# Weight rows laid out in neighbouring pairs, 8 KB per descriptor, in a two-layer mLSTM / attention / mixture-of-experts kernel

## The chip, the cores and the metric

The kernel runs on one core of one Trainium2 chip. The metric is the device time of one execution in microseconds (us), median of 3 runs before the change.

## The reference, cut to what matters

There are 256 tokens of width 1024, all in float32, and two layers. Layer 0 is an mLSTM mixer (a projection to q, k, v, o and gates, then an output projection) and a mixture of experts. Layer 1 projects one shared K/V, then does windowed attention (query and output projections) and a second mixture of experts. After each half there is a LayerNorm of alpha * h + f(h). Of this computation, what the change touches is how the sums over the 1024 (or 512) input features are cut up:

```
proj = x @ w_in                                   # 1024 x 3080, mLSTM
mix  = h @ w_out                                  # 1024 x 1024
k, v = split(x @ w_kv)                            # 1024 x 512
q    = x @ w_q                                    # 1024 x 1024
probs = softmax(t @ w_router)                     # 1024 x 16
for e in range(16):                               # 16 experts, in each of 2 layers
    g, u = split(t @ w_gu[e])                     # 1024 x 1024
    y = (silu(g) * u) @ w_down[e]                 # 512 x 1024
    out += gate[:, e] * y
```

A sum over features may be taken in any order, as long as row r of the weight meets feature r of the other operand.

## The kernel before

**Layout.** A matmul sums over the 128 partitions of both its operands. The 1024 rows of a weight are therefore cut into 8 chunks of 128 (512 rows into 4): row k * 128 + p stands on partition p as chunk k. `big[0..3]` hold four 1024 x 1024 weights (4 MB each), `small[0..1]` two 512 x 1024 weights (2 MB each). The other operand of each product must have feature k * 128 + p on partition p too. It is made by TensorE: `turn` (L379) transposes 128 x 128 blocks of `h` into PSUM, from where ScalarE and VectorE copy them to `hT` (`take_hT`, L868 and L1071); and in the mixture of experts `gather` (L556) multiplies blocks of `h` by a 0/1 matrix `pick` that selects the tokens of two experts, giving `xe`. In both, a block of `h` of 128 neighbouring columns is the stationary operand, the one that a weight load brings into the array. The inner activations `act_g` (64 slots of tokens by 512, kept as 128 x 256) are transposed in the same way in `inner_T` (L590).

**Matmul instructions.** Each float32 matmul of the code shows in the trace as two MATMUL and two LDWEIGHTS instructions; a transpose shows as one of each.

**Weight traffic.** All weight loads are issued by SyncE in program order, in pieces of 1 MB, each with its own semaphore: `load_big` (L198) has four pieces of two chunks, `load_small` (L205) two. In such a piece each partition receives two rows of 4 KB that lie 128 rows apart in memory, as two descriptors of 4 KB. The first 1024 columns of `w_in` (q and k) come in four pieces of 256 columns (L215 to L218), with rows of 1 KB. A piece is issued as soon as the consumer of the buffer's former content is done (`wait_ge` on `gu_done`, `y_done` and the like), so the loads of the experts run about three experts ahead of their use in `big` and one in `small`. TensorE waits for a piece with `wait_big` (L374) or on the semaphores of `small` (L617).

**Order of the experts.** In both layers a turn of four experts is written out (`one_turn`, L637) and runs over four turns. Per expert TensorE does a gate/up product (L582), a transpose (L600), a down product (L619), and per pair of experts a `gather` (L564) and a `scatter` (L631).

**The start.** SyncE issues the two halves of `x`, then `w_in`. ScalarE's sequencer first issues four small DMAs (L865, L866: gate weights and gate biases), and only then reaches the first copies of `take_hT`, for which it loads an activation table. TensorE transposes `x` (L383) and then waits for `hT` and the first piece of `w_in` before the q/k product (L445).

Of the kernel before, what the change touches and what calls it, by code (L numbers as in the profile page):

```python
# [12 lines left out]
P = 128  # L13
NT = SEQ // P
KC = D // P
# [27 lines left out]
def build(nc, x, w_in_a, b_gates_a, mh_norm_a, w_out_a, w_kv_shared, w_q_b, sinks_b, w_out_b,  # L43
          w_router, b_router, w_gu, w_down, ln_g, ln_b, rope, out):
    ctx = ExitStack()
    with ctx:
# [150 lines left out]
        def _(sp):  # L197
            def load_big(n, src):  # L198

                buf, sems, _ = big_at(n)  # L200
                v = src.rearrange("(k p) n -> p k n", p=P)
                for q in range(4):
                    sp.dma_start(buf[:, 2 * q:2 * q + 2, :], v[:, 2 * q:2 * q + 2, :]).then_inc(sems[q], 16)

            def load_small(n, src):  # L205
                buf, sems, _ = small_at(n)
                v = src.rearrange("(k p) n -> p k n", p=P)
                for q in range(2):
                    sp.dma_start(buf[:, 2 * q:2 * q + 2, :], v[:, 2 * q:2 * q + 2, :]).then_inc(sems[q], 16)

# [4 lines left out]
            for q in range(4):  # L215
                sp.dma_start(big[0][:, :, q * 256:(q + 1) * 256],
                             w_in[:, q * 256:(q + 1) * 256].rearrange("(k p) n -> p k n", p=P)
                             ).then_inc(big_in[0][q], 16)  # L218
            load_big(1, w_in[:, 1024:2048])
            load_big(2, w_in[:, 2048:3072])  # L220
            load_big(3, w_out_a[0])
            for l in range(2):
# [10 lines left out]
                if l == 0:  # L233
                    load_dn(0)
                    load_dn(1)
                    sp.wait_ge(qk_done, 8)
                    load_gu(0)
                    sp.wait_ge(v_done, 4)
                    load_gu(1)
                    sp.wait_ge(o_done, 4)  # L240
                    load_gu(2)
                    sp.wait_ge(mix_done, 4)
                    load_gu(3)
                else:


                    sp.wait_ge(y_done, DONE - 1)
                    v = w_kv_shared.rearrange("(k p) n -> p k n", p=P)
                    buf, sems, _ = small_at(D_KV)
                    bv = buf[:, :, :].rearrange("p a (b n) -> p (a b) n", b=2)  # L250
                    for q in range(2):
                        sp.dma_start(bv[:, 4 * q:4 * q + 4, :], v[:, 4 * q:4 * q + 4, :]).then_inc(sems[q], 16)
                    sp.wait_ge(gu_done, DONE)
                    load_big(G_MIX[1], w_q_b[0])
                    load_big(G_MIX[1] + 1, w_out_b[0])
                    load_gu(0)
                    load_gu(1)
                    sp.wait_ge(y_done, DONE)
                    load_dn(0)
                    sp.wait_ge(q_done, 4)  # L260
                    load_gu(2)
                    sp.wait_ge(qT_done, 4)
                    load_dn(1)
                    sp.wait_ge(mix_done, 12)
                    load_gu(3)
# [10 lines left out]
                for e in (4, 5):  # L276
                    buf, sems, _ = big_at(G0 + e)
                    for q in range(4):
                        if q < 3:
                            sp.wait_ge(first_gu, 3 * (2 * l + e - 4) + q + 1)  # L280
                        else:
                            sp.wait_ge(gu_done, DONE + e - 3)
                        sp.dma_start(buf[:, 2 * q:2 * q + 2, :],
                                     w_gu[l, e].rearrange("(k p) n -> p k n", p=P)[:, 2 * q:2 * q + 2, :]
                                     ).then_inc(sems[q], 16)
# [14 lines left out]
                with sp.If(rounds > 0):  # L300
                    sp.wait_ge(s["dve"], 1)
                    with sp.Fori(0, rounds) as j:
                        with sp.Fori(0, EXPERTS) as e:
                            n0 = (j * EXPERTS + e) * (KC + FC)
                            for k in range(KC + FC):

                                sp.wait_ge(s["w_used"], n0 + (k + START))
                                src = (w_gu[l, bass.ds(e, 1), k * P:(k + 1) * P, :] if k < KC else
                                       w_down[l, bass.ds(e, 1), (k - KC) * P:(k - KC + 1) * P, :])
                                sp.dma_start(spill_w, src.rearrange("a p n -> (a p) n")).then_inc(s["w_in"], 16)  # L310

# [59 lines left out]
        def _(pe):  # L371
            mm = nc.tensor.matmul

            def wait_big(n, q, i=0):  # L374

                _, sems, fill = big_at(n)
                pe.wait_ge(sems[q], i * 16 + 16 * fill)

            def turn(src, n, t, j, bank0):  # L379

                for kk in range(4):
                    k = 4 * j + kk
                    last = nc.tensor.transpose(pb[bank0 + 2 * t + j][:, kk * P:(kk + 1) * P],  # L383
                                               src[:, t, k * P:(k + 1) * P], ident[:, :])
                last.then_inc(turned, 1)
# [54 lines left out]
            for g in range(8):  # L440
# [6 lines left out]
                last.then_inc(qk_done, 1)  # L447
            pe.wait_ge(gates_w_in, 64)
            for k in range(KC):
# [39 lines left out]
            for hd in range(M_HEADS):  # L489
# [5 lines left out]
                last.then_inc(num_done, 1)  # L495
            pe.wait_ge(params_in, 16 * 6)
            pe.wait_ge(rows_ready, 1)
# [23 lines left out]

            PAIRS_E = EXPERTS // 2

            def moe(l):
# [31 lines left out]
                def gather(m, P0, ks, bank=1):  # L556

                    for k in ks:
                        if k == 0:
                            pe.wait_ge(pick_ready, P0 + (m + 1))  # L560
                        if k % 4 == 0 and bank == 1:
                            pe.wait_ge(x_sb, (P0 + m) * 2 + (k // 4 - START))
                        for t in range(NT):
                            last = mm(pb[bank][:, (k % 4) * P:(k % 4 + 1) * P], h[:, t, k * P:(k + 1) * P],  # L564
                                      pick[m % 2][:, t, :, :].rearrange("p e s -> p (e s)"),
                                      start=t == 0, stop=t == NT - 1)
                        if k % 4 == 3:
                            last.then_inc(x_got, 1)
# [21 lines left out]
                def inner_T(u, E0, P0):  # L590
# [8 lines left out]
                    for j in range(2):  # L599
                        last = nc.tensor.transpose(pb[3][:, j * P:(j + 1) * P], act_g[u % 2][:, j * P:(j + 1) * P],  # L600
                                                   ident[:, :])
# [77 lines left out]
            def overflow(l):  # L679
# [3 lines left out]
                with pe.If(rounds > 0):  # L683
                    pe.wait_ge(s["dve"], 1)
                    with pe.Fori(0, rounds) as j:
                        with pe.Fori(0, EXPERTS) as e:
                            n = j * EXPERTS + e
                            pe.wait_ge(s["pick"], n + 1)
                            for half in range(2):
                                if half:  # L690
                                    pe.wait_ge(s["xs"], n * 2 + 1)
                                for k in range(4 * half, 4 * half + 4):
                                    for t in range(NT):
                                        last = mm(pb[1][:, (k % 4) * P:(k % 4 + 1) * P], h[:, t, k * P:(k + 1) * P],
                                                  pick[0][:, t, :, :].rearrange("p e s -> p (e s)"),
                                                  start=t == 0, stop=t == NT - 1)
                                last.then_inc(s["x"], 1)
# [10 lines left out]
                            for jj in range(2):  # L708
                                nc.tensor.transpose(pb[3][:, jj * P:(jj + 1) * P], act_g[0][:, jj * P:(jj + 1) * P],
                                                    ident[:, :])  # L710
# [137 lines left out]
        def _(act):  # L848
# [14 lines left out]
            for g in range(2):  # L863
                w4 = w_in_a[0, :, 3072 + g * M_HEADS:3072 + (g + 1) * M_HEADS]
                act.dma_start(w_gate[:, :, 32 * g:32 * g + M_HEADS], w4.rearrange("(k p) n -> p k n", p=P)).then_inc(gates_w_in, 16)  # L865
                act.dma_start(b_gate[32 * g:32 * g + M_HEADS, :],  # L866
# [17 lines left out]
            act.dma_start(rows[0][8:9], mh_norm_a).then_inc(rows_in, 16)  # L884
            act.dma_start(w_rt[:, :, :], w_router.rearrange("(k p) n -> p k n", p=P)).then_inc(params_in, 16)
            act.dma_start(b_rt[:, :], b_router.rearrange("(a n) -> a n", a=1).to_broadcast([P, EXPERTS])).then_inc(params_in, 16)
# [174 lines left out]
        def _(dve):  # L1061
# [46 lines left out]
            for t in range(NT):  # L1108
                take_hT(0, t, 4)
            dve.wait_ge(gates_w_in, 64)  # L1110
            V.tensor_scalar(b_gate[:, :], b_gate[:, :], 1.0 / CAP, None, ALU.mult).then_inc(d2a, 1)
# [53 lines left out]
            def route(l):  # L1165
# [4 lines left out]
                dve.wait_ge(logits, l + 1)  # L1170
                dve.wait_ge(params_in, 16 * 6)
                link(V.reduce_max(r_s[:, 0:2], pb[1][:, 0:32].rearrange("p (t e) -> p t e", t=NT), AX_X))
# [293 lines left out]
```

## Time and profile before

| | |
|---|---|
| median of 3 runs | 772.51 us (772.5 to 772.75) |
| span of the profiled execution (first to last instruction; its own time) | 773.3 us |
| TensorE (PE) busy | 741.0 us, 96% |
| weight loads (PEld) busy, beside PE | 350.1 us, 45% |
| VectorE, ScalarE, GpSimd busy | 171.5, 122.5, 22.3 us |
| DMA | 231.37 MB in 68163 packets, 299 GB/s over the span |

The first row is measured without the profiler, the others come from one profiled execution, whose span is 0.8 us above the median. PE is the matmul side of TensorE, PEld its weight loads, which overlap with matmuls; a busy PE says that it always had a matmul in flight, not that it ran at its peak.

### The profile page before, as it was taken

The page shows a single profiled execution, that of the slowest core. Times are in us where ns is not written, and L with a number is a line of the kernel's source. Part 1 is how long each engine was busy: PE and PEld are TensorE (multiplying, and loading weights), DVE is VectorE, ACT ScalarE, POOL GpSimd, SP SyncE. Part 2 cuts the span into 40 slices and gives each one's busy share as a digit, 9 for nine tenths or more (in the row PEclk, how much of TensorE's full clock was granted, in tenths as well). Part 3 has the DMA queues.
Part 4 walks back from the last instruction along what each step waited for, and adds up shares of the span by engine and source line. Part 5 has one row for each costly group of instructions (what it writes and reads, how often), then busy time and mean ns, then how long its engine had stood idle before and what let it go on. Part 6 is the DMA issues. An engine that isn't in the chain of part 4 may idle for free.

```text
span 773.3 us, 8287 instructions
## 1 busy us (share of the span) xinstructions
PE 741.0 (96%) x3270; PEld 350.1 (45%) x3270; DVE 171.5 (22%) x459; ACT 122.5 (16%) x286; POOL 22.3 (3%) x39
## 2 busy tenths in 40 slices
PE   5999999999999999999999999999999999999994
PEld 5845554554443443443334455455434434434331
DVE  0011121541111111101125354552111111011015
ACT  1122161111111110110122043211111101101002
POOL 3200100000000000000000021100000000000000
PEclk9999989999999999999999999999999999999998
DMA  9999305239699999989659928054979999999931
GB/s 280 390 410 360 146 1 217 81 137 389 237 411 410 409 409 410 409 349 409 256 198 409 409 102 326 1 217 178 366 284 408 410 409 410 410 384 371 389 109 56
DMA packets 68163, 231.37 MB, mean 299 GB/s; under 512 B 7961, under 2 KB 12057, under 8 KB 68130
## 3 DMA queue, kind: packets, MB, share of 16 engines
q1 hardware_dynamic: 63744, 230.70, 76.1%
q10 hardware_dynamic: 4386, 0.21, 0.5%
q8 instruction: 23, 0.38, 0.2%
q14 instruction: 10, 0.08, 0.0%
HBM read 229.85 MB, written 1.05 MB: 299 GB/s over the span
## 4 chain that ended last, share of the span: by engine, by line
PE 92%; DVE 3%; ACT 2%; ACTq 1%; issue 1%; POOL 1%; POOLq 0%; DVEq 0%
PE pb L582 29%; PE pb L413 17%; PE pb L619 15%; PE pb L564 8%; PE pb L631 7%; PE pb L445 4%; PE pb L546 2%; PE pb L751 2%; PE pb L600 1%; PE pb L493 1%; PE pb L532 1%; PE pb L383 1%; PE pb L789 1%; PE pb L390 1%; ACTq L866 1%
## 5 line engine op out<-in xcount | busy, mean ns | idle before, releaser
L413 PE MATMUL pb<-big,hT 128*128 128x512 f32 x320 | 142.5, 599 | 0.8 <-DVE hT L1415 0.8
L619 PE MATMUL pb<-small,bufC 128*64 128x512 f32 x512 | 116.9, 598 | 3.8 <-DVE bufC L1271 3.8
L582 PE MATMUL pb<-big,bufB 128*64 128x512 f32 x512 | 113.1, 594 | 0.0
L582 PE MATMUL pb<-big,hT 128*64 128x512 f32 x512 | 113.0, 594 | 0.0
L413 PEld LDWEIGHTS pb<-big,hT 128*128 128x128 f32 x320 | 59.9, 192 | 71.6 <-issue 69.7
L582 PEld LDWEIGHTS pb<-big,hT 128*64 128x64 f32 x512 | 36.1, 137 | 69.5 <-issue 68.5
L582 PEld LDWEIGHTS pb<-big,bufB 128*64 128x64 f32 x512 | 35.9, 137 | 68.6 <-issue 67.4
L619 PEld LDWEIGHTS pb<-small,bufC 128*64 128x64 f32 x512 | 33.9, 136 | 72.4 <-issue 65.4
L564 PEld LDWEIGHTS pb<-bufC,h 128*128 128x128 f32 x512 | 59.5, 192 | 15.0 <-issue 13.0
L1267 DVE TENSOR_TENSOR bufC<-bufC,pb 128x256 f32<-128x256 f32 x32 | 13.5, 421 | 236.4 <-ACT bufC L968 236.4
L564 PE MATMUL pb<-bufC,h 128*128 128x128 f32 x512 | 63.9, 279 | 0.3 <-DVE bufC L1235 0.3
L631 PE MATMUL pb<-bufB,v_shift 128*128 128x512 f32 x128 | 57.8, 594 | 0.9 <-DVE bufB L1279 0.9
L1279 DVE COPY bufB<-pb 64x512 f32<-64x512 f32 x32 | 21.9, 683 | 161.7 <-PE pb L619 161.7
L964 ACT ACTIVATE bufB<-pb 64x512 f32<-64x512 f32 x32 | 19.0, 593 | 160.9 <-PE pb L619 160.9
L968 ACT ACTIVATE bufC<-pb 128x256 f32<-128x256 f32 x32 | 12.3, 383 | 201.0 <-PE pb L582 201.0
L631 PEld LDWEIGHTS pb<-bufB,v_shift 128*128 128x128 f32 x128 | 23.1, 190 | 24.5 <-issue 23.0
L445 PE MATMUL pb<-hT,big 128*128 128x256 f32 x128 | 29.6, 396 | 3.4 <-ACT hT L872 3.4
L445 PEld LDWEIGHTS pb<-hT,big 128*128 128x128 f32 x128 | 25.4, 199 | 7.5 <-ACT hT L872 3.8
L367 POOL TENSOR_TENSOR bufA<-bufA,st 128x512 f32<-128x512 f32 x8 | 8.1, 1038 | 399.8 <-DVE st L1404 399.8
L600 PEld LDWEIGHTS pb<-ident,bufC 128*128 128x128 f32 x64 | 6.6, 140 | 24.5 <-issue 24.3
L957 ACT ACTIVATE bufB<-pb 128x512 f32<-128x512 f32 x16 | 9.6, 597 | 44.1 <-PE pb L564 44.1
L383 PE MATMUL pb<-ident,h 128*128 128x128 f32 x64 | 10.1, 312 | 5.4 <-DMA h<-in_x 4.4
(206 smaller groups left out, 447.6 us busy)
## 6 DMA issues: line engine op xcount, KB each, us to landing
big<-in_w_gu SPq DMA_DIRECT2D x128, 1024.0 KB, 13.9
small<-in_w_down SPq DMA_DIRECT2D x64, 1024.0 KB, 9.6
big<-in_w_in_a SPq DMA_DIRECT2D x12, 1024.0 KB, 15.5
big<-in_w_out_a SPq DMA_DIRECT2D x4, 1024.0 KB, 18.9
big<-in_w_q_b SPq DMA_DIRECT2D x4, 1024.0 KB, 14.5
big<-in_w_out_b SPq DMA_DIRECT2D x4, 1024.0 KB, 19.2
small<-in_w_kv_shared SPq DMA_DIRECT2D x2, 1024.0 KB, 6.9
h<-in_x SPq DMA_DIRECT2D x2, 512.0 KB, 3.9
```

The source lines that it names most:

```text
L383: last = nc.tensor.transpose(pb[bank0 + 2 * t + j][:, kk * P:(kk + 1) * P], src[:, t, k * P:(k + 1) * P], ident[:, :])
L413: last = mm(pb[bank][:, :], hT[:, k, t * P:(t + 1) * P], w[:, k, c * HALF:(c + 1) * HALF], start=k == 0, stop=k == KC - 1)
L445: last = mm(pb[g // 2][:, (g % 2) * SEQ:(g % 2 + 1) * SEQ], big[0][:, k, g * P:(g + 1) * P], hT[:, k, :], start=k == 0, stop=k == KC - 1)
L546: mm(pb[4 + 2 * t + c][:, :], alpha_i[:, :], h[:, t, c * HALF:(c + 1) * HALF], start=True, stop=False, skip_group_check=True)
L564: last = mm(pb[bank][:, (k % 4) * P:(k % 4 + 1) * P], h[:, t, k * P:(k + 1) * P], pick[m % 2][:, t, :, :].rearrange("p e s -> p (e s)"), s ...
L582: last = mm(pb[0][c * 64:(c + 1) * 64, :].rearrange("p (a n) -> p a n", a=2), xe[u // 2 % 2][:, k, (u % 2) * SLOTS:(u % 2 + 1) * SLOTS], w ...
L600: last = nc.tensor.transpose(pb[3][:, j * P:(j + 1) * P], act_g[u % 2][:, j * P:(j + 1) * P], ident[:, :])
L619: last = mm(pb[2][c * 64:(c + 1) * 64, :], heT[:, j * P + hf * 64:j * P + (hf + 1) * 64], w[:, kk, c * HALF:(c + 1) * HALF], start=(j, hf) ...
L631: ins = mm(pb[4 + 2 * t + c][:, :], back[:, t * P:(t + 1) * P], ye[:, c * HALF:(c + 1) * HALF], start=False, stop=last_one, skip_group_che ...
L751: last = mm(pb[4 + t][:, :], hT[:, k, t * P:(t + 1) * P], kvw[:, k, :], start=k == 0, stop=k == KC - 1)
L964: A(ye[p:p + 64, HALF:2 * HALF], pb[2][64:128, :], ACT.Copy).then_inc(y_sb, 1)
L1279: V.tensor_copy(ye[p:p + 64, 0:HALF], pb[2][0:64, :]).then_inc(y_sb, 1)
```

## The change

A 256-row group of a weight (what was two chunks) is laid out so that partition p holds rows 2p and 2p + 1 of the group. These lie next to each other in memory, so where whole rows are loaded a partition's part of a piece is one run of 8 KB. Chunk 2a + j then has feature 256a + 2p + j on partition p. The other operand follows: the blocks of `h`, of `val` and of `act_g` that are transposed or gathered are taken with every second column (`rows_of`, `half_of`), 128 columns with a step of 8 bytes where they were next to each other. `w_out_b`, whose other operand is the attention's output laid out by head, keeps the old layout (`load_big_by_head`). Pieces that are not whole rows (q/k columns of `w_in`, gate weights, router weights) are now issued as two DMAs of half the size, one for each j, with the counts of the waits adjusted. The K/V weight's rows are 2 KB, so its runs become 4 KB.

```
@@ load_big
-                v = src.rearrange("(k p) n -> p k n", p=P)
+                v = src.rearrange("(q p j) n -> p q j n", p=P, j=2)
                 for q in range(4):
-                    sp.dma_start(buf[:, 2 * q:2 * q + 2, :], v[:, 2 * q:2 * q + 2, :]).then_inc(sems[q], 16)
+                    sp.dma_start(buf[:, 2 * q:2 * q + 2, :], v[:, q]).then_inc(sems[q], 16)
@@ load_small: likewise, for q in range(2); w_gu of experts 4 and 5, w_kv_shared and the overflow path: likewise
@@ first piece of w_in
             for q in range(4):
-                sp.dma_start(big[0][:, :, q * 256:(q + 1) * 256],
-                             w_in[:, q * 256:(q + 1) * 256].rearrange("(k p) n -> p k n", p=P)
-                             ).then_inc(big_in[0][q], 16)
+                for j in range(2):
+                    sp.dma_start(big[0][:, :, q * 256:(q + 1) * 256].rearrange("p (a j) n -> p a j n", j=2)[:, :, j],
+                                 w_in[:, q * 256:(q + 1) * 256].rearrange("(a p j) n -> p a j n", p=P, j=2)[:, :, j]
+                                 ).then_inc(big_in[0][q], 16)
@@ TensorE
+            def rows_of(src, t, k):
+
+                return src[:, t, k // 2 * 256:(k // 2 + 1) * 256].rearrange("p (n j) -> p j n", j=2)[:, k % 2]
@@ turn
-                                               src[:, t, k * P:(k + 1) * P], ident[:, :])
+                                               rows_of(src, t, k), ident[:, :])
@@ gather
-                            last = mm(pb[bank][:, (k % 4) * P:(k % 4 + 1) * P], h[:, t, k * P:(k + 1) * P],
+                            last = mm(pb[bank][:, (k % 4) * P:(k % 4 + 1) * P], rows_of(h, t, k),
                                       pick[m % 2][:, t, :, :].rearrange("p e s -> p (e s)"),
@@ inner_T
+            def half_of(n, j):
+
+                return act_g[n].rearrange("p (n j) -> p j n", j=2)[:, j]
-                        last = nc.tensor.transpose(pb[3][:, j * P:(j + 1) * P], act_g[u % 2][:, j * P:(j + 1) * P],
+                        last = nc.tensor.transpose(pb[3][:, j * P:(j + 1) * P], half_of(u % 2, j),
                                                    ident[:, :])
@@ ScalarE, gate weights (the router's weights w_rt: likewise)
-                act.dma_start(w_gate[:, :, 32 * g:32 * g + M_HEADS], w4.rearrange("(k p) n -> p k n", p=P)).then_inc(gates_w_in, 16)
+                for j in range(2):
+                    act.dma_start(w_gate[:, :, 32 * g:32 * g + M_HEADS].rearrange("p (a j) n -> p a j n", j=2)[:, :, j],
+                                  w4.rearrange("(a p j) n -> p a j n", p=P, j=2)[:, :, j]).then_inc(gates_w_in, 16)
```

On TensorE the instructions stay the same in number and order, except for one register operation per pass through the loop of turns; what changes is the access pattern of the stationary operand. On two queues the instructions change. ScalarE's queue at the start of the program, before the change (`v_shift` is the memory in which the gate weights lie):

```order
L865 DMA v_shift<-in_w_in_a 128x8x4
L866 DMA b_gate<-in_b_gates_a 4x1
L865 DMA v_shift<-in_w_in_a 128x8x4
L866 DMA b_gate<-in_b_gates_a 4x1
L872 ACT_TABLE_LOAD
L872 ACTIVATE hT<-pb 128x4x128 x3
```

and with the change:

```order
L885 DMA v_shift<-in_w_in_a 128x4x4 x2
L887 DMA b_gate<-in_b_gates_a 4x1
L885 DMA v_shift<-in_w_in_a 128x4x4 x2
L887 DMA b_gate<-in_b_gates_a 4x1
L893 ACT_TABLE_LOAD
L893 ACTIVATE hT<-pb 128x4x128 x3
```

Two more DMA issues stand ahead of the copies to `hT`; the bytes are the same. SyncE's queue from its start, before the change:

```order
L212 DMA h<-in_x 128x1024 x2
L216 DMA big<-in_w_in_a 128x8x256 x4
L203 DMA big<-in_w_in_a 128x2x1024 x8
L203 DMA big<-in_w_out_a 128x2x1024 x4
L209 DMA small<-in_w_down 128x2x1024 x4
L203 DMA big<-in_w_gu 128x2x1024 x16
```

and with the change:

```order
L219 DMA h<-in_x 128x1024 x2
L224 DMA big<-in_w_in_a 128x4x256 x8
L203 DMA big<-in_w_in_a 128x2x1024 x8
L203 DMA big<-in_w_out_a 128x2048 x4
L216 DMA small<-in_w_down 128x2048 x4
L203 DMA big<-in_w_gu 128x2048 x16
```

The four q/k pieces are eight half pieces now; the v/o columns of `w_in` still have two runs of 1024 elements to a partition, and the whole-row weights have one of 2048.

## Rows read from the trace of the kernel before

**Rows 1.** The page: busy time, and the span in 40 slices
```profile
PE 741.0 (96%) x3270; PEld 350.1 (45%) x3270; DVE 171.5 (22%) x459; ACT 122.5 (16%) x286; POOL 22.3 (3%) x39
...
PE   5999999999999999999999999999999999999994
...
DMA  9999305239699999989659928054979999999931
GB/s 280 390 410 360 146 1 217 81 137 389 237 411 410 409 409 410 409 349 409 256 198 409 409 102 326 1 217 178 366 284 408 410 409 410 410 384 371 389 109 56
```

**Rows 2.** All waits of PE's matmuls: us in total, times, longest us
```profile
PE pb L383 <- DMA h<-in_x: 4.4, 1, 4.4
PE pb L619 <- DVE bufC L1271: 3.8, 6, 0.9
PE pb L445 <- ACT hT L872: 3.4, 1, 3.4
...
PE pb L564 <- DVE bufC L1235: 0.3, 2, 0.2
```

**Rows 3.** Chain that ended last, one stretch of experts: start us, us, what
```profile
192.09 1.98 PE pb L564 x16
194.08 7.02 PE pb L582 x32
201.09 0.37 PE pb L600 x2
201.46 0.22 PE pb L604 x2
201.68 1.79 PE pb L564 x16
```

**Rows 4.** Groups by shape, weight loads and matmuls: busy us, mean ns | idle
```profile
L564 PE MATMUL pb<-bufC,h 128*128 128x128 f32 x512 | 63.9, 279 | 0.3 <-DVE bufC L1235 0.3
...
L564 PEld LDWEIGHTS pb<-bufC,h 128*128 128x128 f32 x512 | 59.5, 192 | 15.0 <-issue 13.0 <-DVE bufC L1235 2.0
L582 PEld LDWEIGHTS pb<-big,hT 128*64 128x64 f32 x512 | 36.1, 137 | 69.5 <-issue 68.5
...
L383 PEld LDWEIGHTS pb<-ident,h 128*128 128x128 f32 x64 | 8.8, 162 | 9.1 <-issue 5.9 <-DVE h L1101 2.9
...
L600 PEld LDWEIGHTS pb<-ident,bufC 128*128 128x128 f32 x64 | 6.6, 140 | 24.5 <-issue 24.3
...
L383 PEld LDWEIGHTS pb<-ident,bufB 128*128 128x128 f32 x16 | 1.8, 140 | 2.1 <-issue 2.1
```

**Rows 5.** Chain pieces of the denominator matmuls (one moving column each)
```profile
91.76 2.88 PE pb L487 x24
```

**Rows 6.** Windows: us, busy by engine, PEclk, DMA share, GB/s
```profile
0.00:20.00 20.00, 12.25 (x48) 10.58 (x49) 0.84 (x2) 2.86 (x4) 6.98 (x21) 0.91 1.02 279
...
15.00:20.00 5.00, 5.00 (x24) 4.37 (x23) 0.14 (x1) 0.00 (x0) 3.48 (x3) 0.97 1.12 294
26.00:44.00 18.00, 18.00 (x85) 14.50 (x84) 0.00 (x0) 1.97 (x6) 0.00 (x0) 1.00 1.03 411
```

**Rows 7.** SyncE's issues near the end of layer 0, and landings
```profile
353.15 0.88 SPq L209 DMA_DIRECT2D small<-in_w_down  x2
354.07 2.01 SPq L203 DMA_DIRECT2D big<-in_w_gu  x4
...
DMA to landing us min/median/max: 10.9/14.0/17.1
```

**Rows 8.** PE from 376 us: the last expert's gate/up product
```profile
381.12 7.04 PE L582 MATMUL pb<-big,hT 128*64 128x512 f32 x32
```

**Rows 9.** Last w_down of layer 1: issue and landing, and its product
```profile
L209 SPq DMA_DIRECT2D small<-in_w_down x2: 368/420/471, 739.2 to 739.6; - x2
...
DMA to landing us min/median/max: 4.9/5.9/7.0
...
754.72 2.79 PE L619 MATMUL pb<-small,bufC 128*64 128x512 f32 x12 [0.30 <-DVE bufC L1271]
```

**Rows 10.** ScalarE's timeline from 2 us: start us, us, what
```profile
2.37 0.44 ACTq L865 DMA_DIRECT2D v_shift<-in_w_in_a  x1
2.85 0.90 ACTq L866 DMA_DIRECT2D b_gate<-in_b_gates_a  x1
3.78 0.44 ACTq L865 DMA_DIRECT2D v_shift<-in_w_in_a  x1
4.25 4.19 ACTq L866 DMA_DIRECT2D b_gate<-in_b_gates_a  x1
8.47 1.28 ACT L872 ACT_TABLE_LOAD   x1 [8.47 <-issue]
8.60 0.27 ACTq L882 DMA_DIRECT2D bufB<-in_ln_g  x1
```

**Rows 11.** PE at the start, and the q/k pieces' landings
```profile
4.37 3.65 PE L383 MATMUL pb<-ident,h 128*128 128x128 f32 x16 [4.37 <-DMA h<-in_x]
11.39 1.16 PE L445 MATMUL pb<-hT,big 128*128 128x256 f32 x3 [3.38 <-ACT hT L872]
...
DMA to landing us min/median/max: 8.1/12.8/15.4
```

More of the change, by code:

```diff
@@ L200, in load_big, with load_big_by_head @@
                 buf, sems, _ = big_at(n)
+                v = src.rearrange("(q p j) n -> p q j n", p=P, j=2)
+                for q in range(4):
+                    sp.dma_start(buf[:, 2 * q:2 * q + 2, :], v[:, q]).then_inc(sems[q], 16)
+            def load_big_by_head(n, src):
+                buf, sems, _ = big_at(n)
                 v = src.rearrange("(k p) n -> p k n", p=P)
@@ L206, in load_small @@
                 buf, sems, _ = small_at(n)
-                v = src.rearrange("(k p) n -> p k n", p=P)
+                v = src.rearrange("(q p j) n -> p q j n", p=P, j=2)
                 for q in range(2):
-                    sp.dma_start(buf[:, 2 * q:2 * q + 2, :], v[:, 2 * q:2 * q + 2, :]).then_inc(sems[q], 16)
+                    sp.dma_start(buf[:, 2 * q:2 * q + 2, :], v[:, q]).then_inc(sems[q], 16)
             for t in range(NT):
@@ L247, in _ @@
                     sp.wait_ge(y_done, DONE - 1)
-                    v = w_kv_shared.rearrange("(k p) n -> p k n", p=P)
+                    v = w_kv_shared.rearrange("(a p j) n -> p a j n", p=P, j=2)
                     buf, sems, _ = small_at(D_KV)
@@ L251, in _ @@
                     for q in range(2):
-                        sp.dma_start(bv[:, 4 * q:4 * q + 4, :], v[:, 4 * q:4 * q + 4, :]).then_inc(sems[q], 16)
+                        sp.dma_start(bv[:, 4 * q:4 * q + 4, :].rearrange("p (a j) n -> p a j n", j=2),
+                                     v[:, 2 * q:2 * q + 2]).then_inc(sems[q], 16)
                     sp.wait_ge(gu_done, DONE)
                     load_big(G_MIX[1], w_q_b[0])
-                    load_big(G_MIX[1] + 1, w_out_b[0])
+                    load_big_by_head(G_MIX[1] + 1, w_out_b[0])
                     load_gu(0)
@@ L283, in _ @@
                         sp.dma_start(buf[:, 2 * q:2 * q + 2, :],
-                                     w_gu[l, e].rearrange("(k p) n -> p k n", p=P)[:, 2 * q:2 * q + 2, :]
+                                     w_gu[l, e].rearrange("(a p j) n -> p a j n", p=P, j=2)[:, q]
                                      ).then_inc(sems[q], 16)
@@ L307, in _ @@
                                 sp.wait_ge(s["w_used"], n0 + (k + START))
-                                src = (w_gu[l, bass.ds(e, 1), k * P:(k + 1) * P, :] if k < KC else
-                                       w_down[l, bass.ds(e, 1), (k - KC) * P:(k - KC + 1) * P, :])
-                                sp.dma_start(spill_w, src.rearrange("a p n -> (a p) n")).then_inc(s["w_in"], 16)
+                                kk = k if k < KC else k - KC
+                                src = (w_gu if k < KC else w_down)[l, bass.ds(e, 1), kk // 2 * 256:(kk // 2 + 1) * 256, :]
+                                sp.dma_start(spill_w, src.rearrange("a (p j) n -> j (a p) n", j=2)[kk % 2]
+                                             ).then_inc(s["w_in"], 16)
             for t in range(NT):
@@ L376, in wait_big @@
                 _, sems, fill = big_at(n)
-                pe.wait_ge(sems[q], i * 16 + 16 * fill)
+                twice = 16 if n % NG == 0 else 0
+                pe.wait_ge(sems[q], i * 16 + (16 * fill + twice))
+            def rows_of(src, t, k):
+                return src[:, t, k // 2 * 256:(k // 2 + 1) * 256].rearrange("p (n j) -> p j n", j=2)[:, k % 2]
             def turn(src, n, t, j, bank0):
@@ L447, in _ @@
                 last.then_inc(qk_done, 1)
-            pe.wait_ge(gates_w_in, 64)
+            pe.wait_ge(gates_w_in, 96)
             for k in range(KC):
@@ L495, in _ @@
                 last.then_inc(num_done, 1)
-            pe.wait_ge(params_in, 16 * 6)
+            pe.wait_ge(params_in, 16 * 7)
             pe.wait_ge(rows_ready, 1)
@@ L693, in overflow @@
                                     for t in range(NT):
-                                        last = mm(pb[1][:, (k % 4) * P:(k % 4 + 1) * P], h[:, t, k * P:(k + 1) * P],
+                                        last = mm(pb[1][:, (k % 4) * P:(k % 4 + 1) * P], rows_of(h, t, k),
                                                   pick[0][:, t, :, :].rearrange("p e s -> p (e s)"),
@@ L708, in overflow @@
                             for jj in range(2):
-                                nc.tensor.transpose(pb[3][:, jj * P:(jj + 1) * P], act_g[0][:, jj * P:(jj + 1) * P],
+                                nc.tensor.transpose(pb[3][:, jj * P:(jj + 1) * P], half_of(0, jj),
                                                     ident[:, :])
@@ L884, in _ @@
             act.dma_start(rows[0][8:9], mh_norm_a).then_inc(rows_in, 16)
-            act.dma_start(w_rt[:, :, :], w_router.rearrange("(k p) n -> p k n", p=P)).then_inc(params_in, 16)
+            for j in range(2):
+                act.dma_start(w_rt[:, :, :].rearrange("p (a j) n -> p a j n", j=2)[:, :, j],
+                              w_router.rearrange("(a p j) n -> p a j n", p=P, j=2)[:, :, j]).then_inc(params_in, 16)
             act.dma_start(b_rt[:, :], b_router.rearrange("(a n) -> a n", a=1).to_broadcast([P, EXPERTS])).then_inc(params_in, 16)
@@ L1109, in _ @@
                 take_hT(0, t, 4)
-            dve.wait_ge(gates_w_in, 64)
+            dve.wait_ge(gates_w_in, 96)
             V.tensor_scalar(b_gate[:, :], b_gate[:, :], 1.0 / CAP, None, ALU.mult).then_inc(d2a, 1)
@@ L1170, in route @@
                 dve.wait_ge(logits, l + 1)
-                dve.wait_ge(params_in, 16 * 6)
+                dve.wait_ge(params_in, 16 * 7)
                 link(V.reduce_max(r_s[:, 0:2], pb[1][:, 0:32].rearrange("p (t e) -> p t e", t=NT), AX_X))
```

## The prediction, written before the changed kernel ran

> **What bounds the kernel now.** I read the page's busy line and slices first, then the waits, the chain, and the groups by shape. The busy line has TensorE at 741.0 of 773.3 us, and its slices are at 9 tenths or more from the second on [rows 1]. The DMA slices are full as well for long stretches, at 409 to 411 GB/s [rows 1], so at first sight either could be the bound. The waits decide: among all waits of PE's matmuls one alone is for a DMA, 4.4 us for `x` at the very start; the next largest are for VectorE and ScalarE, and none is for a weight [rows 2]. The chain through the experts is matmuls end to end [rows 3]. So in the long middle a microsecond of DMA is worth nothing and a microsecond of TensorE is worth one. This holds only while the loads keep their lead, which I price below.
>
> **Part one: 8 KB runs instead of 4 KB.** This covers `w_out_a`, `w_q_b` and all `w_gu` and `w_down`, some 200 of the 231 MB. What can a longer run gain? The trace has 1 KB pieces at 294 GB/s with 1.12 of the engines' time, and 4 KB pieces at 411 GB/s with 1.03 [rows 6]. Per engine (a sixteenth) that is 18.4 and 25.7 bytes/ns, or 56 ns for 1 KB and 159 ns for 4 KB: 34 ns for each further KB and about 22 ns fixed. An 8 KB run would then take 296 ns, 27.7 bytes/ns, 7% faster. That is an upper bound, since in the window of the 1 KB pieces small transfers of ScalarE's queue share the engines. The lower bound is no gain. The work that hides all of it is the matmuls: the tightest loads are the last ones. The last four `w_gu` pieces of layer 0 are issued from 354.07 us and land 10.9 to 17.1 us after their issue, by about 373 us [rows 7], and their product starts at 381.12 [rows 8]. The last `w_down` of layer 1, issued at 739.2 and 739.6, lands by 746.6 and is used at 754.72, 8 us later [rows 9]. Loads that land earlier release nothing. **Term: 0.** If the cover were gone, in the other direction, 8 us of delay would have to be eaten up first.
>
> **Part two: every second column as stationary operand.** No instruction is added, but 512 gather loads and 144 transposes (64 and 16 of L383, 64 of L600) read with a step of 8 bytes [rows 4]. This is the part that can cost, since it is on TensorE. In the gather the pace is 16 instructions in 1.79 us, 112 ns each [rows 3], and its weight loads are busy for 59.5 of the 63.9 us [rows 4], so they fill the pace. Where a matmul has one moving column and the load of 128 columns alone sets the pace, 24 take 2.88 us, 120 ns each [rows 5]. So a slower load would show in full.
>
> No row has a stationary operand with a step. The bounds come from the nearest rows. A load of 128 float32 columns takes 192 ns and of 64 columns 137 ns [rows 4]: 0.86 ns per column and 82 ns fixed. The lower bound is that the step is free: 0. The upper bound is that a column with a step of 8 bytes costs two: then 110 ns more per load, and 512 of them give 512 x 0.110 = 56 us. Which is nearer? The transposes load 128 neighbouring columns in 140 ns [rows 4], with the same fixed part 58 ns or 0.45 ns per column, so the read side can pass over 4 / 0.45 = 8.8 bytes of a partition per ns. The gather's load with a step has to pass over 8 / 0.86 = 9.3 bytes per ns, practically that rate. I take it as free, **term 0**, with the 56 us kept as the other end. The transposes have no such reserve: at 8.8 bytes/ns a stepped one would load in 82 + 116 = 198 ns. But their pace is 2 in 0.22 us at L604 [rows 3], 110 ns each, so the matmul hides all but some ns: at the 120 ns of [rows 5], 144 x 10 ns = 1.4 us at most. I take 0 for these also, as a transpose pair in the expert loop is prefetched behind 7 us of L582.
>
> For the price of this step there is a rule. The Trainium skill, "SBUF — State Buffer", section "Door 1: the DMA port swizzle", says that the memory is read in 16-byte lines and that two accesses in a line are enough for full speed. By that page a step of two float32 is free and the sum stays as it is; a step of four would not be. No row of this case shows either.
>
> **Part three: more DMA issues at the start.** ScalarE's queue gets two more DMAs ahead of `take_hT`. This is on the path: the issues last from 2.37 to 8.44 us, the table load follows at 8.47 [rows 10], the three copies after it, and TensorE, whose transposes ended at 8.02, stands for 3.38 us until 11.39 [rows 11]. Issues cost 0.27 to 0.44 us where the queue isn't held up [rows 10]. The fourth took 4.19 us, held by the transfers already queued. Their bytes and descriptors stay the same, so I expect the hold to end at about the same moment and to swallow most of the two new issues. Bounds: 0 (all swallowed) and 2 x 0.44 = 0.9 us (none). I take **+0.5 us**. If the hold is by the number of DMAs and not by what they carry, a second hold like the 4.19 could come, less what is already there: up to about +3.6 us. Queued behind these on ScalarE are the copies, and for them waits TensorE, so any of it is paid in full.
>
> On SyncE four issues become eight. The first pair must both have landed before L445. The first piece landed 8.1 us after its issue at 1.7, at 9.9 us, 1.5 us ahead of the start at 11.39 [rows 11]; half a microsecond more of issue fits. **Term: 0.** The router's weights (w_rt) and the second pieces come long before their use. The register operation in TensorE's loop runs in its sequencer, four turns' worth in all. **Term: 0.**
>
> **The sum.** 773.3 (span) + 0 + 0 + 0.5 + 0 = 773.8 us for a profiled execution. The median of the runs stands 0.8 us lower than the span, so **773.0 us** as a median. What a measurement of this kernel can tell from no change is about 0.2%, 1.55 us; the forecast is inside it.
>
> **The rivals.**
> - *The stepped weight load is slower* (slower than before). For it: the gather's loads have no spare time, so 14 ns per load is already 512 x 0.014 = 7 us, and no row shows a step. Against it: the transposes' rate. It decides from 1.55 us / 512 = 3 ns per load. At the full double, 56 us and some 1.4 us of transposes: 830 us. In between, 778 to 800 us. Chance 0.14, half of it near the double.
> - *The start slips* by a second hold on ScalarE's queue: 1.6 to 3.6 us, 774.5 to 776.5 us. For it: the one 0.90 and the one 4.19 us issue [rows 10] were of the tiniest DMA, so the hold isn't about the DMA's own size. Against: the same descriptors drain at the same pace. Chance 0.06.
> - *8 KB runs are slower* than 4 KB ones. The last `w_gu` of layer 0 has 8 us of lead from its landing by 373 [rows 7, 8]; the stream before it is full for some 150 us, so a rate more than 5% lower starts to cost, and 10% lower costs about 7 us in each layer, 787 us. Nothing in the rows speaks for it, the trend from 1 to 4 KB against it. Chance 0.03.
> - *The start gains.* If smaller DMAs free ScalarE's queue before 8.44, the start is held only by the first piece at 9.9 us: 1.5 us less, and up to 1.8 us more if TensorE's clock, granted at 0.91 on average over the first 20 us [rows 6], stays up where it now falls after the idle stretch (0.09 x 20 us); 769.5 to 771 us. Chance 0.07.
> - *The change does what it says and nothing comes of it* is the forecast itself, chance 0.70, its own range 771.5 to 774.5.
>
> **How the numbers follow.** Faster by over 0.2% is the gain case alone, 0.07. Slower is 0.14 + 0.06 + 0.03 = 0.23. The same is 0.70. For the range I take the forecast (0.70), the slipping start (0.06), the near half of the gain (0.04) and the smallest slowdowns of the load, up to 14 ns each (0.03): 770.5 to 780 us holds 0.83.
>
> **What the changed profile would show.** If I am right: the loads of the gather still at 192 ns and 16 gather matmuls in 1.79 us; the packets of the experts 8 KB, with a rate at or somewhat above 409 GB/s and DMA slices that empty earlier; no wait of TensorE for a weight; the first q/k product (L445 before) starting at 11.4 to 12.3 us. Transposes' loads up from 140 ns toward 198 would confirm the reading of the rate without changing the sum. The prediction is wrong if the gather's loads are over 195 ns or its pace over 115 ns, if TensorE's first q/k product starts after 13 us, or if a wait for `big` or `small` appears.

## The result, and the profile after

The changed kernel takes **777.09 us** (777.05 to 777.34, 4 runs) against 772.63 us (772.5 to 772.93) of the kernel before: a ratio of 1.0060, 95% interval 1.0047 to 1.0073. The forecast was 773.0 us with a range of 770.5 to 780. The time lies in the range, but it is slower by 4.5 us where I held "no change" for likeliest.

The busy line, the slices and the packets of the page after, to be laid beside [rows 1]:

```profile
PE 743.8 (96%) x3270; PEld 354.7 (46%) x3270; DVE 171.6 (22%) x459; ACT 122.5 (16%) x286; POOL 22.3 (3%) x39
...
DMA  9999205329599999969659918055789999979921
GB/s 276 378 421 395 112 1 217 142 115 413 225 404 423 422 421 423 421 262 402 254 215 414 422 43 325 1 216 222 321 323 399 422 422 420 423 299 377 383 108 55
DMA packets 42163, 231.37 MB, mean 298 GB/s; under 512 B 8073, under 2 KB 12169, under 8 KB 16530
```

The DMA side did what it was meant to: 42163 packets where there were 68163, and 420 to 423 GB/s in the full slices where there were 409 to 411. The engine that bounds the kernel got more work: PE 743.8 us where it had 741.0. Now the waits of PE's matmuls (us in total, times, longest), as in [rows 2]:

```profile
PE pb L398 <- DMA h<-in_x: 4.4, 1, 4.4
PE pb L638 <- DVE bufC L1294: 3.5, 6, 0.8
PE pb L460 <- ACT hT L893: 2.4, 1, 2.4
```

No wait for a weight appeared or disappeared. So the loss is in the matmuls themselves. Groups by shape (busy us, mean ns | idle), for [rows 4]:

```profile
L583 PE MATMUL pb<-bufC,h 128*128 128x128 f32 x512 | 67.1, 285 | 0.3 <-DVE bufC L1258 0.3
...
L583 PEld LDWEIGHTS pb<-bufC,h 128*128 128x128 f32 x512 | 62.6, 196 | 15.0 <-issue 13.0 <-DVE bufC L1258 2.0
...
L619 PEld LDWEIGHTS pb<-ident,bufC 128*128 128x128 f32 x64 | 10.2, 205 | 24.4 <-issue 24.3
L398 PEld LDWEIGHTS pb<-ident,h 128*128 128x128 f32 x64 | 10.0, 210 | 8.7 <-issue 5.8 <-DVE h L1124 2.6
```

The gather (L564 before, L583 now) went from 63.9 to 67.1 us. The loads of the inner transposes went from 140 to 205 ns, those of the transposes of `h` to 210 ns. The chain in a later stretch of the same kind as [rows 3] (start us, us, what):

```profile
228.84 0.43 PE pb L619 x2
229.27 0.22 PE pb L623 x2
229.49 1.89 PE pb L583 x16
```

Sixteen gather matmuls take 1.89 us for 1.79, a pace of 118 ns for 112, and the pair of inner transposes 0.43 us for 0.37. L623 (L604 before), whose operand has no step, stays at 0.22.

**How the profiled executions compare.** The spans differ by only 2.0 us (775.3 and 773.3) where the medians differ by 4.5. In the timed runs whose span is also on record the device time is 1.7 to 1.9 us above it (777.09 for a span of 775.3). By that difference (an estimate, since this execution's own device time isn't on record) the profiled execution of before, at 773.3, was about 2.5 us longer than its median, and the "0.8 us lower than the span" in my prediction's sum compared a long execution with a usual one. Its TensorE was granted less clock: windows of both kernels, before first (us, busy times, PEclk, DMA share, GB/s):

```profile
90.00:105.00 15.00, 15.00 (x60) 11.33 (x59) 0.88 (x5) 5.60 (x18) 0.00 (x0) 0.77 0.01 2
...
400.00:520.00 120.00, 112.69 (x452) 58.18 (x449) 58.09 (x167) 30.77 (x110) 8.14 (x8) 0.99 0.65 255
```

and after:

```profile
90.00:105.00 15.00, 15.00 (x63) 10.94 (x62) 1.24 (x7) 7.66 (x22) 0.00 (x0) 0.89 0.01 2
...
400.00:520.00 120.00, 112.53 (x453) 58.26 (x450) 58.60 (x169) 30.78 (x110) 8.15 (x8) 1.00 0.62 255
```

These differences fall outside the experts. The first window holds the denominator matmuls (one moving column each) and the products after them. There one line tells the profile of before from that of e1_gather_step2, which runs the same code in this place (start us, us, what); before:

```profile
94.64 8.35 PE pb L493 x24
```

and e1_gather_step2:

```profile
94.32 6.99 PE pb L497 x24
```

The experts' stretches run at a granted clock of 1.00 in every execution, and where two kernels have the same code there, they repeat to 0.01 us. So below I compare them by themselves: stretch A from the first gather of layer 0 to the first K/V matmul, stretch B from the first gather of layer 1 to its last scatter. Their ends are rows of each timeline, such as these four of the changed kernel:

```profile
165.12 4.04 PE L583 MATMUL pb<-bufC,h 128*128 128x128 f32 x32 [0.16 <-DVE bufC L1258]
412.06 1.13 PE L770 MATMUL pb<-small,hT 128*128 128x512 f32 x2 [0.77 <-ACT hT L893]
524.72 2.50 PE L583 MATMUL pb<-bufC,h 128*128 128x128 f32 x19 [0.16 <-DVE bufC L1258]
761.11 3.70 PE L650 MATMUL pb<-bufB,v_shift 128*128 128x512 f32 x8 [0.47 <-DVE bufB L1302]
```

A is 412.06 - 165.12 = 246.94 us, B is 761.11 - 524.72 = 236.39 us.

### The profile page after: what moved, and what is told of

The parts are those of the page before. It is cut to its first block, busy times and chain, and to the rows that moved or that the text cites. A ratio compares the mean times of both kernels' runs of the same rounds, so it can differ in the third digit from the quotient of the medians.

```text
span 775.3 us, 8294 instructions
## 1 busy us (share of the span) xinstructions
PE 743.8 (96%) x3270; PEld 354.7 (46%) x3270; DVE 171.6 (22%) x459; ACT 122.5 (16%) x286; POOL 22.3 (3%) x39
## 2 busy tenths in 40 slices
DMA packets 42163, 231.37 MB, mean 298 GB/s; under 512 B 8073, under 2 KB 12169, under 8 KB 16530
## 4 chain that ended last, share of the span: by engine, by line
PE 91%; DVE 4%; ACT 2%; POOL 1%; issue 1%; ACTq 1%; POOLq 0%; DVEq 0%
PE pb L601 29%; PE pb L428 16%; PE pb L638 15%; PE pb L583 8%; PE pb L650 7%; PE pb L460 4%; PE pb L565 2%; PE pb L770 2%; PE pb L619 2%; PE pb L551 1%; PE pb L398 1%; PE pb L508 1%; PE pb L405 1%; POOL bufA L377 1%; PE pb L808 1%
## 5 line engine op out<-in xcount | busy, mean ns | idle before, releaser
L583 PEld LDWEIGHTS pb<-bufC,h 128*128 128x128 f32 x512 | 62.6, 196 | 15.0 <-issue 13.0
L583 PE MATMUL pb<-bufC,h 128*128 128x128 f32 x512 | 67.1, 285 | 0.3 <-DVE bufC L1258 0.3
L619 PEld LDWEIGHTS pb<-ident,bufC 128*128 128x128 f32 x64 | 10.2, 205 | 24.4 <-issue 24.3
L619 PE MATMUL pb<-ident,bufC 128*128 128x128 f32 x64 | 15.9, 329 | 0.0
```

Of the source, the lines that this page charges most:

```text
L583: last = mm(pb[bank][:, (k % 4) * P:(k % 4 + 1) * P], rows_of(h, t, k), pick[m % 2][:, t, :, :].rearrange("p e s -> p (e s)"), start=t == ...
L619: last = nc.tensor.transpose(pb[3][:, j * P:(j + 1) * P], half_of(u % 2, j), ident[:, :])
```

## The experiments

What each run gave; "against before" is the ratio to runs of the kernel before on the same chip, with its 95% interval. The first row has the lowest and the highest of that kernel's medians over the chips; A and B come from the one profiled execution of each:

| run | median us | against before | A us | B us |
|---|---|---|---|---|
| before | 772.43 to 773.05 | | 244.50 | 233.95 |
| changed kernel | 777.09 | 1.0060 (1.0047 to 1.0073) | 246.94 | 236.39 |
| e1_gather_step2 | 777.33 | 1.0056 (1.0039 to 1.0073) | 246.07 | 235.52 |
| e2_inner_step2 | 774.94 | 1.0023 (1.0012 to 1.0034) | 245.37 | 234.84 |
| e3_pairs_no_step | 773.01 | 1.0005 (0.9995 to 1.0015) | 244.50 | 233.95 |
| e4_gather_step4 | 835.53 | 1.0814 (1.0796 to 1.0832) | 275.64 | 265.09 |
| e5_gather_step8 | 837.84 | 1.0853 (1.0834 to 1.0871) | 276.83 | 266.30 |
| e6_copies_first | 771.78 | 0.9988 (0.9977 to 0.9999) | 244.49 | 233.95 |
| e7_both_steps | 779.10 | 1.0093 (1.0079 to 1.0108) | 246.94 | 236.39 |
| e8_after_again | 777.23 | 1.0072 (1.0057 to 1.0086) | 246.94 | 236.39 |
| e9_step_on_write | 777.57 | 1.0071 (1.0052 to 1.0089) | 246.72 | 236.17 |

**e1_gather_step2.** Is the gather's loss its operand's step, or the 8 KB traffic beside it?

```
@@ before, gather
-  h[:, t, k * P:(k + 1) * P]
+  rows_of(h, t, k)          # every second column, as in the changed kernel
```

> The kernel before, with the step of two columns in the gather's stationary operand alone; everything else, the weights' layout too, stays, so the experts see permuted features and the output is not the reference's. Theory (the stepped load costs a little more each): weight loads 196 ns instead of 192, 16 gathers in 1.88 us instead of 1.79, 512 x 6 ns = 3.1 us more, a median of about 775.7 us. Rival (the 3.2 us of the gather in the changed kernel came from its DMA traffic, the 8 KB runs, landing in the same memory): 772.6 us and 1.79 us, as before.

Its gather rows are the changed kernel's, though its DMAs are those of before:

```profile
L568 PE MATMUL pb<-bufC,h 128*128 128x128 f32 x512 | 67.1, 285 | 0.3 <-DVE bufC L1239 0.3
...
L568 PEld LDWEIGHTS pb<-bufC,h 128*128 128x128 f32 x512 | 62.6, 196 | 15.0 <-issue 13.0 <-DVE bufC L1239 2.0
```

A and B grew by 1.57 us each, together 3.14 us for 512 loads, 6.1 ns per load. The step alone does it, and the rival falls. The whole time rose by 4.5 us, with an interval of 3.0 to 5.6, which holds the 3.1. The profiled execution also has two long stretches outside the experts, which e7 comes back to.

**e2_inner_step2.** The same question for the inner transposes.

```
@@ before, inner_T
-  act_g[u % 2][:, j * P:(j + 1) * P]
+  act_g[u % 2].rearrange("p (n j) -> p j n", j=2)[:, j]
```

> The kernel before, with the step in the transposes of the inner activations alone (64 transposes); the down product sees permuted features, so the output is not the reference's. Theory: their loads go from 140 to about 200 ns, and since each pair stands between products that fill the engine, the pair's stretch in the chain goes from 0.37 to 0.43 us, 32 times 0.06 = 2 us, median about 774.6 us. Rival (my prediction's: the transposes' matmuls hide their loads): at most 0.3 us, 772.9 us.

```profile
L600 PE MATMUL pb<-ident,bufC 128*128 128x128 f32 x64 | 15.9, 330 | 0.0
L600 PEld LDWEIGHTS pb<-ident,bufC 128*128 128x128 f32 x64 | 10.2, 206 | 24.4 <-issue 24.3
```

A and B grew by 0.87 and 0.89 us, 1.8 us together, and the median by 2.1. The loads are not hidden: each loads 66 ns longer, and each pair takes some 0.06 us longer, the growth of one of its two loads.

**e3_pairs_no_step.** The other half of the change by itself: all its DMAs, no step.

```
@@ changed kernel
     def rows_of(src, t, k):
-        return src[:, t, k // 2 * 256:(k // 2 + 1) * 256].rearrange("p (n j) -> p j n", j=2)[:, k % 2]
+        return src[:, t, k * P:(k + 1) * P]
     def half_of(n, j):
-        return act_g[n].rearrange("p (n j) -> p j n", j=2)[:, j]
+        return act_g[n][:, j * P:(j + 1) * P]
```

> The changed kernel with all its DMAs (8 KB runs, split first pieces), but TensorE reads 128 neighbouring columns again everywhere; the operands no longer match, so the output is not the reference's. Theory (the step is the whole cost, and the start gains 1.1 us): the start at 10.3 us stays, gather 1.79 us for 16, median about 771.5 us. Rival one (8 KB runs cost something, or the loop's added register operation does): 773 us or more. Rival two (the 8 KB runs gain on their own): under 770.5 us.

Its gather loads are those of before, its packets and its rate from 250 to 290 us (the last number, GB/s) those of the changed kernel:

```profile
L583 PEld LDWEIGHTS pb<-bufC,h 128*128 128x128 f32 x512 | 59.5, 192 | 15.0 <-issue 13.0 <-DVE bufC L1258 2.0
...
DMA packets 42163, 231.37 MB, mean 300 GB/s; under 512 B 8073, under 2 KB 12169, under 8 KB 16530
...
250.00:290.00 40.00, 40.00 (x209) 18.09 (x208) 5.33 (x13) 4.23 (x9) 0.00 (x0) 1.00 1.01 421
```

A and B are those of before to 0.01 us, so in the experts the 8 KB runs and the added register operation neither cost nor gain anything, while the traffic is visibly faster. The median of 773.01 stands at the edge of my rival one, but before ran at 772.84 on this chip: the ratio is 1.0005, and its interval leaves room for 0.4 us less and 1.2 us more. The expected gain at the start didn't come (the q/k product began at 10.88 us, not 10.3); e6 takes that up.

**e4_gather_step4 and e5_gather_step8.** What is the price of a step made of? The same place as in e1, but the 128 columns are every fourth one of a group of 512 (`j=4`, 16 bytes) and every eighth one of all 1024 (`j=8`, 32 bytes).

> As e1_gather_step2, but with a step of four columns, 16 bytes; again the experts see permuted features. Theory one (the load has a rate in bytes of the partition passed over, some 9 bytes/ns, which two columns just reach): 128 x 16 / 9 = 228 ns over the fixed 82, loads about 310 ns, 16 gathers in 3.7 us, 512 x 0.116 = 59 us more, about 832 us. Theory two (any step costs a fixed 6 ns per load): 775.7 us, as with a step of two. The Trainium skill, SBUF - State Buffer, section Door 1, has lines of 16 bytes and a penalty when each access goes to a new one, which speaks for theory one without giving the size.

> As e4_gather_step4, but with a step of eight columns, 32 bytes; the experts see permuted features. With steps of 1, 2 and 4 the gather's pace was 112, 118 and 233 ns per matmul. Theory one (what counts is 16-byte pieces of a partition touched: 1.82 ns each, so 0.91 ns per column at a step of two and 1.82 at four): a step of eight touches as many pieces as a step of four, pace 233 ns, about 835 us. Theory two (what counts is the bytes passed over, some 9 per ns): 128 x 32 / 9 = 455 ns, about 950 us.

Pieces of the chain of both, 16 gathers each (start us, us, what), with a step of four:

```profile
241.86 3.73 PE pb L568 x16
```

with a step of eight:

```profile
240.63 3.80 PE pb L568 x16
```

That is 233 and 238 ns per matmul, 112 with no step, 118 with a step of two. In e4 the fixed price fell, and theory one came close (62.7 us more for 59 forecast). But bytes passed over and 16-byte pieces touched say much the same up to a step of four. e5 tells them apart: twice the bytes passed over cost 2% more, not 95%. The number of separate 16-byte pieces of a partition that the load touches fits all four: a step of four touches 128 and takes 233 ns, 1.82 ns each; a step of two touches 64, 117 ns by this price, 118 measured; a step of eight touches 128 again and takes 238, 2% more than this price says, for which I have no reason. With no step 32 pieces would take 58 ns, and the load is bound by its columns, at 112. The Trainium skill, "SBUF — State Buffer", section "Door 1: the DMA port swizzle", tells of such 16-byte lines and of a penalty where each access goes to a new one. These runs agree in kind, and a step of two was nearly free as the Trainium skill has it (free), but only nearly: the load's own 112 ns cover almost all of the 117.

**e6_copies_first.** Does anything at the start count, and is there a version that beats both?

```
@@ before, ScalarE
-  act.wait_ge(gate_zero, 2); the four DMAs of the gate weights and biases
   for t in range(NT):
       take_hT(0, t, 4)
+  act.wait_ge(gate_zero, 2); the four DMAs of the gate weights and biases
```

> The kernel before, with ScalarE's four gate DMAs moved behind the first copies to hT in its queue; output as the reference's. Theory (the issues ahead of the copies set the start): the table load starts at 1 us, the copies follow the transposes at 8.1 to 8.7 us, and the q/k product starts when the first piece of w_in has landed, at about 9.9 us instead of 10.3 to 11.4; 0.5 to 1.5 us less, about 771.5 us. Rival (the start is held by the first piece, or the clock's drop takes the gain back): 772.6 us.

Its ScalarE and TensorE at the start:

```profile
0.97 1.28 ACT L866 ACT_TABLE_LOAD   x1 [0.97 <-PEq L1450]
...
8.99 3.33 PE L445 MATMUL pb<-hT,big 128*128 128x256 f32 x7 [1.01 <-DMA big<-in_w_in_a]
```

The q/k product starts at 8.99 us, held by the first piece of `w_in` alone. The median is 0.65 us below that of before, ratio 0.9988 with an interval of 0.9977 to 0.9999. It is the fastest kernel of the study among those that compute what the reference does, if only just told from before. The product starts 2.4 us earlier than in [rows 11], but the median gains 0.65 us. About half of those 2.4 us is spread between executions of the same code: the product of e1, with the start of before, began at 10.31 us. And the profiled execution of e6 is one of its shorter ones (770.59 us, 1.2 below its median), so its 8.99 can't be set against the 0.65 us directly.

**e7_both_steps and e8_after_again.** Do the parts add up? e7 is before with the edits of e1 and e2 together, e8 the changed kernel again, on the same chip.

> The kernel before, with the step of two columns in the gather and in the transposes of the inner activations, and its own weights' layout; the features no longer match, so the output is not the reference's. Theory (the two steps are nearly all of the change's loss and add up): 32 x 0.10 + 32 x 0.06 = 5.0 us over before, about 777.7 us, the time of the changed kernel. Rival (e1's 4.5 us were more than the gather's 3.2 because a part of the loss is elsewhere and comes once): 775 to 776 us.

> The changed kernel itself, on the same chip as e7_both_steps. Theory: the same as e7_both_steps within 0.15%, since what it has more (8 KB runs, the split first pieces, 10 groups of transposes of h and val at 0.08 us each, 0.8 us) is worth less than 1 us; 777 to 778.5 us. Rival (the 8 KB runs give back a part that e3 could not show): over 1 us faster than e7_both_steps.

A and B of e7 are those of the changed kernel to 0.01 us: the two steps are the whole loss in the experts. But e7 is 1.9 us slower than e8 as a whole, outside what I expected. The two profiled executions, 1.3 us apart, show where such a difference lies. The q/k product, whose matmuls and loads are the same in both kernels, took in e7 (start us, us, what)

```profile
10.37 30.88 PE pb L449 x128
```

and in e8

```profile
10.52 29.58 PE pb L460 x128
```

That is 1.3 us. The attention, from the first K/V matmul to the first gather of layer 1, took 113.38 us in e7 (526.23 - 412.85) and 112.64 in e8, 0.74 us less, with a granted clock of 0.99 in e7's window from 400 to 520 us against 1.00. Smaller stretches on which e8 is the longer one, the stepped transposes among them, take the rest back. Such differences follow no edit. Over all eleven profiled executions the q/k product took 29.58 us in seven and 30.13 to 30.88 in four (e1, e3, e6, e7), and the attention 112.4 to 114.1 us, the longest in e1, e2 and e5. Why is open: from 10 to 15 us the profile shows a granted clock of 1.00 in e7 and 0.66 in e8, and still e7's product took longer.

**e9_step_on_write.** Can an engine with idle time pay instead? The silu and the product write `act_g` in the paired order, so `inner_T` reads neighbours.

```
@@ changed kernel
+  act_w = [act_g[n].rearrange("p (j n) -> p n j", j=2) for n in range(2)]
-  A(act_g[u % 2], pb[0][:, 0:256], ACT.Silu)
+  A(act_w[u % 2], pb[0][:, 0:256].rearrange("p (n j) -> p n j", j=2), ACT.Silu)
@@ and the same in the product, V.tensor_tensor
@@ half_of
-  return act_g[n].rearrange("p (n j) -> p j n", j=2)[:, j]
+  return act_g[n][:, j * P:(j + 1) * P]
```

> The changed kernel, but the inner activations are written to their tile in the paired order by ScalarE and VectorE, so that the transposes of inner_T read 128 neighbouring columns; output as the reference's. The gather keeps its step. Theory (the step costs where TensorE reads it, and ScalarE and VectorE have idle time): the two stretches of the experts shrink from 246.9 and 240.3 us to 246.0 and 239.4, as in e1_gather_step2, 1.8 us less than the changed kernel, about 775.4 us. Rival (the silu and the product take longer with a stepped write, and TensorE's transposes wait for them): a new wait of the transposes for VectorE, and 777 us or more.

Its waits and groups:

```profile
PE pb L639 <- DVE bufC L1295: 5.1, 6, 1.2
...
L992 ACT ACTIVATE bufC<-pb 128x256 f32<-128x256 f32 x32 | 19.9, 622 | 201.0 <-PE pb L602 201.0
L1291 DVE TENSOR_TENSOR bufC<-bufC,pb 128x256 f32<-128x256 f32 x32 | 19.5, 611 | 245.3 <-ACT bufC L992 245.3
L620 PE MATMUL pb<-ident,bufC 128*128 128x128 f32 x64 | 13.9, 298 | 0.0
```

The transposes are back at 13.9 us. But the silu takes 622 ns for 383 and the product 611 for 421. In the loop that is covered; at the first and last experts of each layer six down products wait for this chain, and four of the six waits grew by 0.4 us each, 3.5 to 5.1 us in all. A and B gained 0.22 us each instead of 0.87, and the median (777.57) shows no gain over the changed kernel. Each of my theories held in part: the transposes' gain is there, and so is the longer wait that eats most of it.

## Why the prediction was right, and where it was wrong

**What bounds the kernel: right.** TensorE; a faster DMA was worth nothing that e3 could tell.

**Part one, 8 KB runs, term 0: right.** The rate rose by 2.9%: 421 GB/s in a window of the experts (250 to 290 us) against 409, well inside the bound of 7%. The loads landed 8 us and more before anything waited for them, so the gain went off the critical path.

**Part two, the stepped operand, term 0: this is the step that failed.** I bounded it from 0 to 56 us and took 0, by the row of the transposes' loads. The mechanism and the direction of the risk were there (a slower load shows in full, it decides from 3 ns per load); the choice of zero was off. Measured: 6.1 ns per load, 3.1 us, by the step alone (e1). The argument was "9.3 bytes/ns are needed, practically the 8.8 that are shown": read strictly, 9.3 is more than 8.8, and 128 x 8 / 8.8 = 116 ns against the 110 of the load was the measured answer. I rounded away the very 5% that made the difference. The rate in bytes is itself only a stand-in for the count of pieces, as e5 shows; at a step of two they say the same.

**The transposes, term 0: wrong too.** Their loads came out at 205 to 210 ns where I had worked out 198. But I took the inner pair to be prefetched behind the gate/up product. It costs 0.06 us per pair, 1.8 us in all (e2), more than the 0.64 us that my 10 ns each would have given for these 64. [rows 3] could have told me: the inner pair took 0.37 us there and the pair of L604 0.22, so a load of the inner pair was already showing. Why the pair's loads are not taken earlier wasn't tested. Of the ten groups of eight transposes of L398, most of those in the chain show 0.95 us where they had 0.87; at 0.08 us each all ten are at most 0.8 us. My 10 ns per transpose gave the same for these 80.

**Part three, the start, term +0.5: not seen.** The table load that follows ScalarE's first issues began at 8.47 us in the profile of before and at 7.39 in e1, which has the same four DMAs ahead of it; in the four executions with six it began at 7.36 (the changed kernel) to 7.96 (e3). The start varies by a microsecond between executions, and two more issues can't be told in it. That fits the hold swallowing them, as I had thought likely, but doesn't show it.

**The sum.** 3.1 + 1.8 in the experts is 4.9, with up to 0.8 for the other transposes 5.7 us. Measured are 4.5 and, in e8, 4.8 us, with intervals of 3.6 to 5.6 and 4.4 to 6.6. The first interval ends just short of the 5.7, the second holds it. The microsecond by which the parts exceed the medians is no more than the q/k product or the attention alone varies by between executions (e7); it isn't traced further.

**The chances.** I gave "slower" 0.23 and the stepped load 0.14, half of it near the double. The outcome was the smallest form of that rival, 6 ns per load where I had named 14 as a small case, together with a term for the transposes that I had put at nothing. That the time lies in the range is in part luck: the range reached up to 780 for the slipping start and for slowdowns of up to 14 ns, to which I gave 0.06 and 0.03, and not for the case that I held for likely, whose own range ended at 774.5.

## What to carry to other kernels

Before making descriptors longer, look at who waits for the DMA: where no matmul does, a transfer that is 3% faster is worth nothing, and any cost that it puts on the bound engine is all that is left. In a chain of float32 matmuls with 128 moving columns like this gather, the weight load sets the pace, so its access pattern counts to the nanosecond: with 512 of them, 6 ns are 3 us. When a bound says "practically equal", put the difference into the sum.

## What the runs showed of the hardware that I had not expected

The pace of weight loads of 128 float32 columns was 112, 118, 233 and 238 ns for steps of 1, 2, 4 and 8 columns. The larger of two prices, one by columns and one of 1.82 ns by 16-byte pieces, fits these four; other steps were not tried. A transpose's load, which took 140 ns for 128 neighbouring columns where the gather's took 192, is the one that a step of two slowed most: to between 205 and 210 ns for the inner activations and `h`. On 256 columns, ScalarE's silu with a write that alternates between two places 512 bytes apart took 622 ns for 383. VectorE's product, which both read and wrote its tile in that order, took 611 ns for 421.
